# Walking the last three slabs of a down projection one output quarter at a time

## The reference

```python
h2 = rms_norm(x, norm_ffn_pre[l])
up = causal_depthwise_conv(h2 @ w_up[l], conv_w[l], conv_b[l])
g, v = jnp.split(up, 2, axis=-1)
ff = (jax.nn.gelu(g, approximate=True) * v) @ w_down[l]   # (256, 2816) @ (2816, 1024)
x = x + rms_norm(ff, norm_ffn_post[l])
```

## Time and profile before

| | |
|---|---|
| median of 3 runs | 965.12 us (964.76 to 965.45) |
| profiled execution, first to last instruction (span) | 963.8 us |
| TensorE busy | 940.9 us, 98% of the span |
| VectorE busy | 579.0 us, 60% |
| ScalarE busy | 495.6 us, 51% |
| GpSimd busy | 97.8 us, 10% |
| mean granted TensorE clock | 0.999 of full speed |

### The profile page before, as it was taken

One profiled execution on the slowest core, in us unless ns is written; L12 is line 12 of the kernel. 1 busy time (PEld: TensorE's weight loads), 2 busy tenths in 40 slices (PEclk: granted clock), 3 DMA queues, 4 the chain that ended last, 5 costly groups with the idle time before them and its releaser, 6 DMA issues.

```text
span 963.8 us, 16050 instructions
## 1 busy us (share of the span) xinstructions
PE 940.9 (98%) x6428; PEld 862.5 (89%) x6428; DVE 579.0 (60%) x758; ACT 495.6 (51%) x725; POOL 97.8 (10%) x145
## 2 busy tenths in 40 slices
PE   6999999999999999999989999999999999999997
PEld 6998887887987999988879989999999799999885
DVE  5664666554644666643455438767487578887643
ACT  5764545534654555433354346666543566656531
POOL 7202122210001000000030006001000200000000
PEclk9999999999999999999999999999999999999999
DMA  7865523225433656555536554444455376665631
GB/s 246 264 222 175 175 94 118 95 88 175 140 122 97 192 184 196 184 176 191 201 99 219 175 175 132 148 159 154 162 185 179 110 188 188 188 176 175 216 133 45
DMA packets 134803, 157.54 MB, mean 163 GB/s; under 512 B 3751, under 2 KB 113565, under 8 KB 134749
## 3 DMA queue, kind: packets, MB, share of 16 engines
q1 hardware_dynamic: 133085, 151.78, 49.1%
q0 software_dynamic: 1056, 3.93, 1.1%
q10 hardware_dynamic: 608, 1.06, 0.3%
HBM read 155.71 MB, written 1.05 MB: 163 GB/s over the span
## 4 chain that ended last, share of the span: by engine, by line
PE 94%; DVE 2%; ACT 1%; DMA 1%; POOL 1%; issue 0%; SPq 0%; DVEq 0%; POOLq 0%; ACTq 0%
PE tb L549 18%; PE tb L550 17%; PE tb L551 17%; PE acc L549 11%; PE acc L551 10%; PE acc L550 10%; PE tb L627 1%; PE acc L732 1%; PE tb L689 1%; DMA raw<-in_w_in 1%; PE tb L688 1%; ACT junk L1071 1%; PE tb L824 0%; PE tb L908 0%; PE acc L955 0%
## 5 line engine op out<-in xcount | busy, mean ns | idle before, releaser
L1467 DVE TENSOR_TENSOR wlo<-raw,whi 128x2048 fp32r<-128x2048 f32 (+1 forms) x143 | 327.2, 2291 | 252.7 <-ACT whi L1044 252.5
L549 PE MATMUL tb<-xhi,whi 128*128 128x256 f32 x1256 | 357.7, 285 | 1.1 <-DVE xlo L1480 0.8
L551 PE MATMUL tb<-xhi,wlo 128*128 128x256 f32 x1256 | 355.3, 283 | 0.0
L550 PE MATMUL tb<-xlo,whi 128*128 128x256 f32 x1256 | 355.3, 283 | 0.0
L1044 ACT ACTIVATE whi<-raw 128x2048 fp32r<-128x2048 f32 (+1 forms) x143 | 272.2, 1908 | 140.9 <-PE acc L551 117.2
L549 PEld LDWEIGHTS tb<-xhi,whi 128*128 128x128 f32 x1256 | 240.9, 192 | 2.3 <-issue 1.7
L550 PEld LDWEIGHTS tb<-xlo,whi 128*128 128x128 f32 x1256 | 241.0, 192 | 0.1
L551 PEld LDWEIGHTS tb<-xhi,wlo 128*128 128x128 f32 x1256 | 240.9, 192 | 0.0
L549 PE MATMUL acc<-whi,hid_hi 128*128 128x512 f32 x128 | 50.6, 396 | 0.0
L550 PE MATMUL acc<-wlo,hid_hi 128*128 128x512 f32 x128 | 50.6, 396 | 0.0
L551 PE MATMUL acc<-whi,hid_lo 128*128 128x512 f32 x128 | 50.6, 395 | 0.0
(11 more groups left out here) (325 smaller groups left out, 1411.0 us busy)
## 6 DMA issues: line engine op xcount, KB each, us to landing
raw<-in_w_in SPq DMA_DIRECT2D x42, 1024.0 KB, 5.2
raw<-in_w SPq DMA_DIRECT2D x32, 1024.0 KB, 5.2
raw<-in_w_up SPq DMA_DIRECT2D x44, 512.0 KB, 5.0
raw<-in_w_down SPq DMA_DIRECT2D x22, 512.0 KB, 4.0
raw<-in_w_xkv SPq DMA_DIRECT2D x8, 1024.0 KB, 5.4
raw<-in_w_out SPq DMA_DIRECT2D x8, 1024.0 KB, 4.8
raw<-in_w_mem_kv SPq DMA_DIRECT2D x4, 1024.0 KB, 5.1
raw<-in_w_xq SPq DMA_DIRECT2D x4, 1024.0 KB, 5.1
```

Of the source, the lines that this page charges most:

```text
L549: pe.matmul(o, a_hi, b_hi, start=start, stop=False)
L550: pe.matmul(o, a_hi, b_lo, start=False, stop=False)
L551: return pe.matmul(o, a_lo, b_hi, start=False, stop=stop)
L1467: dve.tensor_tensor(wlo[:, n % RING, :m], raw[:, n % RING, :m], whi[:, n % RING, :m].bitcast(F32), ALU.subtract).then_inc(lo_ready, 1)
```

## The change

TensorE no longer finishes slab 8, then 9, then 10. It takes slabs 0 to 7 as before. Then it holds slabs 8, 9 and 10 in the three buffers and walks the quarters: quarter 0 of slabs 8, 9 and 10, then quarter 1 of the three, and so on. The matmuls are the same 72; their order and the places of waits and signals change. No other engine's program changes.

```diff
             pe.wait_ge(dve_emptied, dve_evacs[first["w3"] + 3])
-            for j in range(NT2 // 2):
+            held = range(NT2 // 2 - RING, NT2 // 2)
+            for j in range(held[0]):
                 pe.wait_ge(cvs["lo"], 2 * j + 2)
                 row_slab(first["wd"] + j, vhi, vlo, 2 * j, NT2)
+            pe.wait_ge(cvs["lo"], NT2)
+            for q, (t, c) in enumerate(QUARTERS):
+                for j in held:
+                    n = first["wd"] + j
+                    if q == 0:
+                        split_ready(n)
+                    b_hi, b_lo = slab(whi, n, 2), slab(wlo, n, 2)
+                    a, v = slice(t * P, t * P + P), slice(c * 512, c * 512 + 512)
+                    for k in range(2):
+                        kt = 2 * j + k
+                        last = mm3(acc[:, c, t, :], vhi[:, kt, a], vlo[:, kt, a], b_hi[:, k, v], b_lo[:, k, v],
+                                   False, kt == NT2 - 1)
+                    if q == 3:
+                        last.then_inc(slab_done, 1)
+                if q < 3:
+                    last.then_inc(part_done, 1)
```

## The result

The changed kernel takes 966.83 us (median of 20 runs, 966.22 to 968.05), the kernel before 965.19 us in 20 runs beside it: 1.64 us more, a ratio of 1.0016 with a 95% interval of 1.001 to 1.0021. That is under 0.2%, so by the bound set ahead it counts as the same, though the whole interval lies above 1 and its upper end a little beyond 0.2%. The forecast was 966.7 us. In one experiment, e4, a single execution took 2130 us, more than twice all others; it was the profiled one (TensorE busy for 2114 us instead of 941, VectorE for 584 instead of 579, the granted clock 1.00; the cause is open), so the tail is not read from it and e10 repeats it.

What follows compares the result with a forecast made beforehand. TensorE, busy 98% of the span, was taken to bound the kernel, with the tail behind its last matmul. A new wait of +1.95 us and a tail of -0.41 gave 965.12 + 1.54 = 966.7 us, range 965.7 to 967.6 (8 in 10).

Steps and rivals of the forecast that it cites:

- What bounds the end: Kernel's end: unbroken matmuls, then quarter 3's sum of squares, GpSimd, VectorE's two additions and a store, a tail of some 6 us.
- Term 1: Before slab 10's matmuls in quarter 0: TensorE waits for VectorE's split and restarts, costing +1.95 us.
- Term 2: Behind the last matmul: GpSimd's L447 no longer runs beside added(0), taking 0.30 instead of 0.71 us, -0.41 us.
- What costs nothing: In the changed stretch: the single cvs["lo"] wait, late slab_done signals, queues and unchanged matmul and weight-load counts add no time.
- (a): In the tail: no shortening, L447 stays at 0.71 us while the wait is paid, 967.1 us; chance 0.13.
- (b): In the new TensorE gap: the clock falls, up to 14.0 us more, 980.7, if all 60 remaining matmuls slow; chance 0.04.
- (c): At slab 10: its split is ready in time, no new wait, only the shorter tail, 964.7 us; chance 0.03.
- (d): In the tail: it shrinks by more, giving 3.9 us back, to come out below 963.2 on the span; chance 0.02.
- The sum: Over the whole kernel: +1.95 - 0.41 = +1.54 us, median 966.7 us, 0.16% slower, called the same.
- The chance of 0.25 for slower: Whole kernel slower by over 0.2%: 0.15 from the forecast, 0.06 from (a) and 0.04 from (b).

Runs made afterwards that it cites:

- e4: Kernel before the change, with VectorE's additions for the first token half moved ahead of gained(2) and gained(3) in the last norm: 965.65 us beside 965.51.
- e10: The same kernel as e4, run again because its profile fell in the overlong execution: 964.74 us beside 966.09, ratio 0.9991.
- e3: Changed kernel with slab 10 split into the projection input's buffers, so it need not wait for slab 7's: 964.92 us, ratio 0.9997 to the kernel before.
- e1: Changed kernel holding only slabs 9 and 10 for the walk by quarters, slab 8 finished first: 964.63 us, ratio 0.9995 to the kernel before.
- e2: Changed kernel taking quarters 0 and 1 of slabs 8 and 9 before slab 10: 964.78 us, ratio 0.9995 to the kernel before.
- e5: Changed kernel with added(0) held back until the last sum of squares is there, to run beside L447: 968.39 us beside 965.79, ratio 1.0027.
- e6: Changed kernel with three more ScalarE activations ahead of slab 10's rounding, lengthening TensorE's gap: 971.13 us beside 965.79, ratio 1.0057.
- e7: Changed kernel with nine more ScalarE activations ahead of slab 10's rounding, lengthening TensorE's gap: 974.86 us, ratio 1.0094 to the kernel before.
- e9: Kernel of e6 with 30 filler transpositions keeping TensorE busy during its wait for slab 10: 968.51 us beside 966.09, ratio 1.0034.
- e8: Kernel before with two-slab walks ending w2, w3 and wd, and the filler behind w3 cut from 28 to 16 transpositions: 965.07 us beside 966.09.
- e12: Kernel of e8 with the 28 filler transpositions put back behind w3: 964.09 us beside 965.58, ratio 0.9984 to the kernel before.
- e11: Kernel of e8 with ScalarE, VectorE and GpSimd doing the first token half first in the norm behind w3: 963.77 us beside 965.58, ratio 0.9979.

## Why the prediction was right

**What bounds the end.** The chain was right: matmuls, then quarter 3's sum of squares, GpSimd, two additions and the stores, before and after.

**Term 1, the new wait.** Forecast +1.95 us, measured +1.92. The gap shown is 1.69 us; the rest is the restart. The two parts of the restart differ a little from the rows they came from: the first matmul starts 0.15 us behind VectorE's end at 944.49, as in the earlier trace rows; the second follows after 0.30 us, not 0.33. Slab 8's first matmul started at 939.99 and not at 940.7, and the last one at 958.47 and not near 959.2; with the 0.70 us from ahead taken off, both are as forecast. The cause stands by e3 (the buffer gone, the wait gone) and e1 and e2 (slab 10 wanted later, the wait gone).

**Term 2, the tail.** Forecast -0.41 us, measured -0.42. That it was L447 is shown by e10, with the order of one engine changed and nothing else, and the reverse by e5. The prediction named the rule of the Trainium skill, page "SBUF — State Buffer", section "Who interferes with whom"; the rows of e10 and e5 agree with it (0.30 us beside an instruction that reads PSUM, 0.85 beside one that reads two operands in SBUF). Why the hardware does this no run here shows; only that it depends on which VectorE instruction runs beside. One point of the picture was too coarse: L447 was said to wait for `added`, both instructions. In the rows of before it started beside the second of them, so they could not tell one from two, and e5, which expected 1.5 us from the pair, measured 0.85.

**What costs nothing.** The late `slab_done` signals and the single wait for `cvs["lo"]` left no trace: TensorE has one wait in the stretch.

**The rivals.** (a), no shorter tail, fell with L447's 0.30 us. (b), the clock, did not come in the profiled execution, at 1.00 on both sides of the gap. But there was luck in it. Its chance of 0.04 rested on one passage of the 1.96 us gap behind `w3` in one execution, and behind the same gap the clock fell in the profiles of e1, e2 and e6. How often it fell in the new gap in the changed kernel's other 19 runs no row shows. The prediction priced this rival up to 14.0 us; the rows give 1.1 to 1.2 us behind the gap of 1.96 and 1.5 to 2.1 behind those of e6 and e7, since the clock comes back within 3.4 to 4.4 us of work. Even 1.2 us in most executions would have put the change at +2.7 us, 0.28%, beyond 0.2%. The Trainium skill, page "TensorE: Matmul & The Clock Gate", section "HAM oscillation — how this bites in real kernels", warns of waits that let the clock fall; e6 and e9 agree with it at a gap of 3.67 us. (c), no wait, is refuted by the gap itself; (d) would have needed 3.9 us.

**The sum.** +1.54 forecast, +1.50 in the profile, +1.64 between medians, an interval of about 1.0 to 2.0 us around it. The range of the terms was put at 966.1 to 967.3; its lower end comes out at 965.12 + 1.70 - 0.65 = 966.2, which changes nothing. The chance of 0.25 for slower stood for a case that did not come; with an interval up to 1.0021 it was no idle figure.

## What to carry to other kernels

When work is regrouped so that a result is complete earlier, write down for each buffer when it is wanted before and after: here the last slab moved forward from 48 to 12 steps, against a split that ends some 4.5 us behind the first, and that alone turned a gain of 0.4 us into a loss of 1.5. Hold only as much as the gain needs (two slabs gave the same tail as three), and look for the queue behind it: the same walk in front of the norm behind `w3` gave nothing until the other engines' order let the first half go first. A wait on TensorE is dearer than it looks once the clock falls, by 1.1 to 2.1 us here, and one profile in which the clock held does not show that it will hold in the next execution. A filler is not worth cutting where the start of what follows it doesn't move (e8).

## What was not expected of the hardware

The length of a gap does not settle whether the clock falls. Behind `w3` TensorE is idle for 1.96 us (1.97 in e7), in code that e1, e2 and e6 share with the kernel before. In the profiles of before, of the change and of e3, e5, e7, e9 and e10 this gap passed at a granted clock of 1.00, and the 32 transpositions behind it took 4.30 or 4.31 us. In those of e1, e2 and e6 the clock fell behind it, and they took 5.44, 5.52 and 5.49 us. From e1:

```profile
764.37 5.44 PE L627 MATMUL tb<-dg,h 128*128 128x128 f32 x32 [1.96 <-POOL dg L440]
...
765.00:770.00 5.00, 5.00 (x33) 5.00 (x31) 3.52 (x12) 4.20 (x15) 1.48 (x3) 0.66 0.33 105
```

The run times fit this. Of the 33 runs of the kernel before that stand beside e1 to e4, 20 have a mean granted clock of 0.999 and a median of 965.1 us, 13 have 0.996 to 0.998 and a median of 966.1. Each gap length of the experiments has one profile: 1.69 us (the change), 1.85 (e12) and 2.41 us (e11) passed at 1.00, while behind or in those of 3.16 (e8), 3.67 (e6) and 7.63 us (e7) the clock fell. That is no threshold. What decides besides the length was not tried.

Nor does the fall come at a fixed place. In e6 three matmuls ran 0.23 us apart behind 3.67 us of idle time before the steps went to 0.427; in e7 the clock was down inside the gap, 0.50 from 946 to 951.

GpSimd, it seems, got in between two VectorE instructions that stood directly behind each other, and was held up by each in turn (e5, one profile: L447 0.85 us and L448 0.84 us, where they take 0.30 and 0.56 alone).
